# The first layer's modulation computed by TensorE in four parts, and half of its projection taken row by row

## What is computed

```
c_act = jax.nn.silu(c)                                  # c is one row of 1024
mod = c_act @ w_ada[l] + b_ada[l]                       # w_ada[l] is 1024 x 3072
shift, scale, gate = jnp.split(mod, 3, axis=-1)
h = rms_norm(x, g_pre[l]) * (1.0 + scale) + shift
proj = h @ w_in[l]                                      # w_in[l] is 1024 x 3072
u_a, b_a, c_a, gate_a, u_p, gate_p = parts of proj, 512 columns each
y_a = b_a * causal_depthwise_conv(c_a * u_a, w_conv[l]) * silu(gate_a)
y_p = causal_multiscale_pool(u_p, w_pool[l], pool_scale[l]) * silu(gate_p)
x = x + gate * rms_norm(concat(y_a, y_p) @ w_out[l], g_post[l])
```

## Time and profile before

| | |
|---|---|
| median of 3 runs | 1285.74 us (1283.43 to 1291.79) |
| the profiled execution's own time | 1283.65 us |
| its span in the profile | 1281.9 us |
| TensorE busy | 1246.6 us, 97% |
| DVE / ScalarE / POOL busy | 69% / 50% / 13% |
| HBM read | 234.92 MB, 184 GB/s over the span |

### The profile page before, as it was taken

One profiled execution on the slowest core, in us unless ns is written; L12 is line 12 of the kernel. 1 busy time (PEld: TensorE's weight loads), 2 busy tenths in 40 slices (PEclk: granted clock), 3 DMA queues, 4 the chain that ended last, 5 costly groups with the idle time before them and its releaser, 6 DMA issues.

```text
span 1281.9 us, 19570 instructions
## 1 busy us (share of the span) xinstructions
PE 1246.6 (97%) x7756; PEld 1109.8 (87%) x7756; DVE 887.8 (69%) x931; ACT 641.3 (50%) x825; POOL 171.9 (13%) x217
## 2 busy tenths in 40 slices
PE   3899999999999999989999999999999999999998
PEld 2899899888888899978988888888889998988887
DVE  5779666676666767987766667666667787766665
ACT  2445545554444456855544444444446675644442
POOL 8400100088200120000100001000001221200000
PEclk9999899999999999999999999999999999999999
DMA  9897495455556462314555654655554444455551
GB/s 361 262 324 270 158 326 185 145 197 183 186 189 196 121 215 66 132 67 131 187 182 189 196 186 144 227 197 191 182 186 164 148 147 157 151 187 196 196 196 66
DMA packets 166816, 236.88 MB, mean 185 GB/s; under 512 B 5140, under 2 KB 146592, under 8 KB 164704
## 3 DMA queue, kind: packets, MB, share of 16 engines
q1 hardware_dynamic: 165920, 235.09, 54.9%
q0 software_dynamic: 816, 0.89, 0.3%
q10 hardware_dynamic: 16, 0.00, 0.0%
HBM read 234.92 MB, written 1.05 MB: 184 GB/s over the span
## 4 chain that ended last, share of the span: by engine, by line
PE 85%; DVE 6%; DMA 4%; ACT 2%; POOL 1%; issue 1%; DVEq 0%; ACTq 0%; POOLq 0%
PE acc L2185 23%; PE acc L2187 12%; PE acc L2221 5%; PE acc L2222 5%; PE acc L2223 5%; PE acc L2203 4%; PE acc L2204 3%; PE acc L2205 3%; DVE wlo L1349 2%; DMA raw<-in_w_ada_dram 2%; PE acc L2239 2%; PE acc L2593 2%; DMA raw<-in_w_in_dram 2%; PE acc L2241 2%; PE acc L2240 2%; PE acc L2122 2%
## 5 line engine op out<-in xcount | busy, mean ns | idle before, releaser
L1349 DVE TENSOR_TENSOR wlo<-raw,whi 128x2048 fp32r<-128x2048 f32 (+1 forms) x199 | 453.8, 2283 | 199.7 <-ACT whi L745 198.7
L745 ACT ACTIVATE whi<-raw 128x2048 fp32r<-128x2048 f32 (+1 forms) x199 | 378.1, 1904 | 184.3 <-PE acc L2223 113.1
L2185 PE MATMUL acc<-hT,whi 128*128 128x512 f32 x1280 | 320.2, 392 | 0.5 <-ACTq L826 0.5
L2185 PEld LDWEIGHTS acc<-hT,whi 128*128 128x128 f32 x1280 | 232.4, 189 | 43.9 <-issue 0.7
L2187 PEld LDWEIGHTS acc<-hT,wlo 128*128 128x128 f32 x1280 | 174.6, 190 | 12.5
L2187 PE MATMUL acc<-hT,wlo 128*128 128x256 f32 x1280 | 178.5, 282 | 0.0
L2221 PE MATMUL acc<-whi,sT_hi 128*128 128x512 f32 x320 | 125.0, 391 | 0.0
L2222 PE MATMUL acc<-wlo,sT_hi 128*128 128x512 f32 x320 | 125.0, 390 | 0.0
L2223 PE MATMUL acc<-whi,sT_lo 128*128 128x512 f32 x320 | 124.5, 389 | 0.0
L2203 PE MATMUL acc<-whi,hT 128*128 128x256 f32 x416 | 120.2, 289 | 1.1 <-DVE hT L1423 1.1
L2204 PE MATMUL acc<-wlo,hT 128*128 128x256 f32 x416 | 117.6, 283 | 0.0
(11 more groups left out here) (324 smaller groups left out, 1950.6 us busy)
## 6 DMA issues: line engine op xcount, KB each, us to landing
raw<-in_ffn_w_in_dram SPq DMA_DIRECT2D x88, 1024.0 KB, 5.1
raw<-in_ffn_w_out_dram SPq DMA_DIRECT2D x44, 1024.0 KB, 5.0
raw<-in_w_ada_dram SPq DMA_DIRECT2D x24, 1024.0 KB, 5.9
raw<-in_w_in_dram SPq DMA_DIRECT2D x24, 1024.0 KB, 5.9
raw<-in_diff_w_in_dram SPq DMA_DIRECT2D x12, 1024.0 KB, 5.2
raw<-in_nsa_w_in_dram SPq DMA_DIRECT2D x10, 1024.0 KB, 5.3
raw<-in_w_out_dram SPq DMA_DIRECT2D x8, 1024.0 KB, 4.9
raw<-in_nsa_cmp_w_dram SPq DMA_DIRECT2D x4, 1024.0 KB, 5.5
```

The source lines that it names most:

```text
L745: nc.scalar.activation(whi[:, w % SPL, 0:n], raw[:, r % RAW, 0:n], ACT.Copy).then_inc(hi_ready, 1)
L1349: nc.vector.tensor_tensor(wlo[:, w % SPL, 0:n], raw[:, r % RAW, 0:n], whi_f[:, w % SPL, 0:n], ALU.subtract).then_inc(raw_done, 1)
L2185: nc.tensor.matmul(o, hi[:, kt, cs], hT[:, :, kt, :], start=kt == 0, stop=False)
```

## The change

**Modulation.** The eight items of w_ada[0] become four pairs of items ("pair", f, half). Pair f holds the shift and scale columns of feature tiles 2f and 2f + 1; each half holds 512 of the 1024 rows, and is loaded by two transfers of 512 KB. pair_product multiplies a half by c on TensorE: 16 fp32 matmuls, each with a 128 x 128 piece of raw as the weights and one column of c as the moving operand. DVE no longer touches these items; pass_pair on DVE waits until TensorE is through with them and counts raw_done. pair_modulation makes shift1 and gain1 of two feature tiles.

**Projection.** The six chunks of u_p, gate_a and gate_p (columns 1536 to 3071) become eight "row" items of 128 rows by 1536 columns (0.75 MiB). For each feature tile kt, row_high and row_low (row_last for the last) add its product to six PSUM banks: two of 128 tokens by 512 columns, four with two column tiles by 256 tokens. clear_gates first writes zeros to four of these banks with 4 fp32 matmuls of 512 columns. features(f) on ScalarE and features_lo(f) on DVE make hT_hi and hT_lo for two feature tiles at a time. Then the other six chunks (COLS1) run by columns as before, with pooled means, mixing and gate between them, now written out one by one on each engine. acc_ada for layer 0 keeps only the gate.

**Around it.** x is the first transfer. b_ada and g_pre are loaded by ScalarE's queue and turned early; the other parameters (16 transfers on POOL's queue in place of 18) are turned later (turn_params). xn of the first 128 tokens is made by ScalarE, that of the others by DVE. keep_clock is gone. The second layer and all behind it run as before.

```diff
+    items = pair(0) + rows(0) + pair(1) + rows(1, 2) + pair(2) + rows(3, 4) + pair(3) + rows(5, 6, 7)
+    side = {0: [("gate", 0, 1)], 1: [("gate", 0, 2)], 2: [("gate", 0, 3)], 3: [("ada", 1, 1)], 4: [("ada", 1, 2)]}
...
+            def pass_pair():
+
+                for _ in range(2):
+                    if raw_at[0]:
+                        dve.wait_ge(raw_done, raw_at[0])
+                    raw_at[0] += 1
+                    dve.wait_ge(pair_used, sum(it[0] == "pair" for it in items[0:raw_at[0]]))
+                    dve.sem_inc(raw_done, 1)
...
+            def pair_product(f, half):
+
+                r = items.index(("pair", f, half))
+                pe.wait_ge(raw_landed[r % RAW], landed_value(r))
+                rv = raw[:, r % RAW, :].rearrange("p (k s n) -> p k s n", k=4, s=2)
+                if half == 0:
+                    nc.tensor.matmul(acc[:, 6, 4 * f:4 * f + 4], zeros[:, :], ones[:, 0:4], start=True, stop=False)
+                for j in range(4):
+                    for k in range(4):
+                        kt = 4 * half + k
+                        ins = nc.tensor.matmul(acc[:, 6, 4 * f + j:4 * f + j + 1],
+                                               rv[:, k, j // 2, (j % 2) * P:(j % 2 + 1) * P], cact[:, kt:kt + 1],
+                                               start=False, stop=j == 3 and kt == KD - 1)
+                ins.then_inc(pair_used, 1)
...
+            def row_high(kt, low):
+
+                w = w_at[("row", kt)]
+                hi = whi[:, w % SPL, 0:ROWN]
+                src = hT_lo if low else hT_hi
+                if low:
+                    pe.wait_ge(feat_ready, kt + 1)
+                else:
+                    pe.wait_ge(feat_hi, kt + 1)
+                    pe.wait_ge(hi_ready, w + 1)
+                for tt in range(TT):
+                    nc.tensor.matmul(acc[:, 4 + tt, :], src[:, kt, tt * P:(tt + 1) * P], hi[:, CW:2 * CW],
+                                     start=kt == 0 and not low, stop=False)
+                for c, b in ROW_GATES:
+                    for ft in range(2):
+                        at = (c - 6) * CC + ft * P
+                        nc.tensor.matmul(acc[:, b, ft * T:(ft + 1) * T], hi[:, at:at + P], src[:, kt, :],
+                                         start=False, stop=False)
...
+            def clear_gates():
+
+                pe.wait_ge(xT_ready, 2)
+                pe.wait_ge(xT0_ready, 2)
+                for _, b in ROW_GATES:
+                    nc.tensor.matmul(acc[:, b, :], zeros[:, :], xn[:, 1, 0:512], start=True, stop=False)
```

More of the change, by code:

```diff
@@ L2275, in sum_modulation @@
                 ins.then_inc(mod_ps, 1)
-            def keep_clock(n):
-                for _ in range(n):
-                    nc.tensor.matmul(acc[:, 7, :], ones[:, :], xn[:, 1, 0:512], start=True, stop=True)
+            def clear_gates():
[3 more added lines that the diff above has]
+                    nc.tensor.matmul(acc[:, b, :], zeros[:, :], xn[:, 1, 0:512], start=True, stop=False)
+            pair_product(0, 0)
@@ L2283, in _ @@
             turn(0, 0)
             turn(0, 1)
-            pe.wait_ge(raw_done, KD - 2)
-            keep_clock(3)
-            pe.wait_ge(shift_rows, 1)
-            for j in range(16):
-                if j == 8:
-                    pe.wait_ge(raw_done, KD)
-                ins = nc.tensor.matmul(acc[:, 6, j:j + P], acc_ada[:, j * P:(j + 1) * P], ones[:, :],
-                                       start=True, stop=True)
-            ins.then_inc(mod_ps, 1)
-            keep_clock(2)
+            pair_product(0, 1)
@@ L2326, in _ @@
                     if n == 9:
[L2328 to L2332 removed]
+                        spread_gate(l)
                 n_proj += 12
```

525 lines of the change are left out of this document (385 added, 140 removed).

## The result

The changed kernel takes 1337.53 us (median of 4 runs, 1329.08 to 1340.37) against 1284.83 us for the kernel before beside it: ratio 1.040, 95% interval 1.034 to 1.046. It is slower, by more than the range allowed.

What follows compares the result with a forecast made beforehand. The prediction took TensorE to bound the first layer from its first projection matmul on. Floor 3.9, waits 10 and clock 18 made 32 us on 1283.65, so 1316 us; range 1296 to 1328.

Steps and rivals of the forecast that it cites:

- the signs named for the trace: First layer: strings of 3.4 us or more, clock near 0.5, DMA idle 14 to 21 us; wrong if outputs before 125.
- The floor: Row phase without waits at 2.4 GHz: first column chunk starts at 79.3 us, 3.9 us later than break-even.
- the waits: Row phase, three raw slots: waits move the first column chunk from 79.3 to 89.3 us, 10 us.
- The clock: Row phase: one-column strings put TensorE at 1.2 GHz, also for following work; between 0 and 20 us, 18 taken.
- The walk at the lower clock: Row phase stepped through at half-clock prices: first column chunk starts at 109.9 us, 34.5 us after break-even.
- covered, but with no chunk in hand: After the rows: 19 loads, 55 us, hide under 42 + 22.7 us of TensorE work; cost 0 to 8, 0 taken.
- The break-even point: First column chunk must start at 75.4 us, 42 us before the old projection's end at 117.4, to lose nothing.
- Rival (4): Column phase after the rows: three items between the first two column chunks, DMA sets the pace, +42 to +55; chance 0.06.
- (1): Row phase: clock stays high through the strings, apart from the cold start; +12 to +20 us; chance 0.14.
- (2): Row phase: the waits are covered too; +4 to +12 us, no measurable difference; chance 0.09.
- (3): Row phase: string weights load under other work, a string under 1 us; up to 27 us faster, 1257; chance 0.03.

Runs made afterwards that it cites:

- the wide version: The changed kernel with each string's 16 one-column matmuls replaced by 4 matmuls of 512 columns, and 512-column clearing matmuls: 1322.00 us, ratio 1.030.
- the joined one: The changed kernel with pairs multiplied on DVE, pair 0's sums first, two column chunks loaded first, DVE's and ScalarE's orders mended: 1302.85 us, before two gate loads moved.
- both queues mended: The changed kernel with DVE's and ScalarE's work reordered in the column phase: 1332.63 us; with side loads and their DVE work cut to 64 columns too, 1323.82 us.
- the last version above: The changed kernel with pairs multiplied on DVE, orders of loads, DVE and ScalarE mended, and two gate loads moved into the row phase: 1301.48 us, ratio 1.013.

## Why the prediction was wrong

The sign was right, the size was not: +32 forecast, +45.4 in the profiled execution, +53 in the median. Of the signs named for the trace, DMA was idle from 14 to 21 us, and the output matmuls came at 151.8 us; pair 0 ended at 23.7 us, not 27, and the first row matmul stood at 28.66, not 32.

- **The floor and the waits (+3.9, +10): right in sum at the full clock, not what the changed kernel spent.** In the wide version the start was 92.9 us, and 89.2 without its 3.7 us of wide clearing (an estimate), against 89.3 walked. That they meet so closely is partly luck: it was idle for 8.0 us from 9 us to the start, not 10, and its first string took 4.84 us, not 3.6. In the changed kernel TensorE was idle for 3.7 us in that time, since the slower strings covered the waits.
- **The clock (+18 of 20): the mechanism was right, its size changes with the execution.** The walk at the lower clock gave 109.9 us. The seven other kernels of the same row phase started at 104.3 to 110.5, the profiled execution of the changed one at 101.26, since pair 0's second string and pair 1 stayed at the full clock there. So the row phase costs 26 to 35 us, 32 forecast. Against the wide version without its wide clearing, the clock alone gives 12 to 21 us (an estimate). That the strings of pair 1 "may keep the clock" was so in three of ten traces; that they do for standing apart was not.
- **The step that failed is "covered, but with no chunk in hand ... which may cost 0 to 8 us; I take 0".** It measured 19.4 us. It set 19 items "at 2.9 us each", 55 us, against 64.7 us of TensorE. 2.9 us is the distance of two loads at the start, where they are only multiplied by DVE and no split stands in the chain. In the stretch, taking two loads out made it 6.7 us shorter in one version and 4.5 in the joined one, 3.3 and 2.2 us a load. By the first of these the four loads more than before are 13 us (an estimate); cutting transfer and DVE work of the twelve side loads took out 10.0 us, and with both queues mended 14.2. So the loads were not covered. The 69.5 us of the kernel before for 18 loads, 3.86 us each, are no price of a load, since TensorE was busy for 68.9 of them: they say only that a load took no more.
- **The break-even point carried the same error.** "42 us" of TensorE work behind the first column chunk was right (42.6 us busy in the last version above, at the full clock; 46.3 in the changed kernel at 0.93). But equal work left for TensorE isn't equal work left for the slots: at 75.4 us the kernel before had four more loads behind it.
- **Rival (4), "Starved columns",** came nearest, with +42 to +55, and got 0.06. Its price was the walk at the lower clock with 8 more for the loads. The DMA share of 84 to 86% spoke for it: 18 loads kept the transfers busy for 0.82 of 69.5 us, so 22 would fill all of it (an estimate). But the transfers alone did not set the pace: cut to a busy share of 0.49 they left 85.0 us. The stream puts two items, not three, between the first two column chunks. Rivals (1) and (2) fell with the strings, (3) as its own condition said: a pass cost 0.11 us or more, not under 0.09.

The Trainium skill, page "TensorE: Matmul & The Clock Gate", section "Why this matters for your kernels", has the clock stay up where no long idle gap lies between bursts. The strings speak against it as the one row did: no gap, and the clock neither rose (44 us of them) nor held in seven of ten traces. In the other direction it fits: the wide matmuls kept the clock at 0.99 through a row phase whose longest wait is 1.1 us.

What stays open: why pair 1 keeps the clock in one execution and not in another; and what makes the last 5 us of the stretch, which show as 1.8 us more of waits and 3.4 us more of busy TensorE at a lower clock (0.94 against 0.98).

## What to carry to other kernels

When work is moved ahead in a kernel fed through a few slots, count at the break-even point what is left for every resource, loads too, and price a load where it passes the same chain, not from a start where one engine takes it; the quotient of a stretch that another engine bounds is only an upper limit. An engine that waits for loads is free only for work shorter than the gap, priced at the clock it has there: here a string was 6.8 us and not 3.4, against loads 2.9 us apart. If a wait goes and the stretch stays as long, ask what each slot must pass before trying a third order.

## What the runs showed of the hardware

- One-column fp32 matmuls with new weights each cost 0.11 to 0.12 us a pass at the full clock and 0.213 at half. Busy without a gap, strings of them and transposes did not get quicker in 44 us (the granted clock is shown as 1.00 there, ahead of its first record, though each pass took 0.213 us).
- A string of 32 such passes that began at the full clock took 4.1 to 5.2 us in place of 3.7 in seven of ten traces, and the next string ran wholly at half (6.8 us); in three traces both kept the clock. Strings of 8 and 16 passes (1.0 and 1.9 us) kept it at 1.00.
- fp32 matmuls that move 512 columns over one column of weights take the same time (3.59 us for 4) and kept the clock at 0.99 in the same places.
